# Three low parts and one block sum ahead of the first weight quad move from VectorE to GpSimd, and the order of the rest changes

## The reference, cut to what matters

```
def swiglu(h, wg, wu, wd):
    return (jax.nn.silu(h @ wg) * (h @ wu)) @ wd
...
xp = xp + swiglu(rmsnorm(xp, norm_ffn[l]), w_ff_gate[l], w_ff_up[l], w_ff_down[l])
```

## Time and profile before

| what | value |
|---|---|
| median of 3 runs | 2334.61 us |
| the profiled execution's span | 2334.1 us |
| its own time beside the span | no separate figure is given; the runs lie 0.8 us below to 1.3 us above the span |
| PE busy | 2267.3 us, 97% |
| DVE busy | 1309.4 us, 56% |
| POOL busy | 976.5 us, 42% |
| ACT busy | 862.2 us, 37% |

### The profile page before, as it was taken

One profiled execution on the slowest core, in us unless ns is written; L12 is line 12 of the kernel. 1 busy time (PEld: TensorE's weight loads), 2 busy tenths in 40 slices (PEclk: granted clock), 3 DMA queues, 4 the chain that ended last, 5 costly groups with the idle time before them and its releaser, 6 DMA issues.

```text
span 2334.1 us, 39824 instructions
## 1 busy us (share of the span) xinstructions
PE 2267.3 (97%) x15066; PEld 2183.7 (94%) x15066; DVE 1309.4 (56%) x2354; ACT 862.2 (37%) x1686; POOL 976.5 (42%) x988
## 2 busy tenths in 40 slices
PE   7999999999999899999999999999999989999997
PEld 7999998888999899999999999988889989999997
DVE  7996553334237835727589865433332387275374
ACT  4015233444213534625420152334441246255252
POOL 4544454232563342333455545533326623333231
PEclk9999999999999999999999999999999999999998
DMA  5251121111222222222234411211113312223121
GB/s 182 93 188 65 51 73 55 37 41 32 90 99 82 73 91 73 85 78 80 68 135 140 128 57 60 67 48 41 41 32 105 106 60 87 81 82 100 64 85 61
DMA packets 70564, 187.84 MB, mean 80 GB/s; under 512 B 19824, under 2 KB 22480, under 8 KB 69392
## 3 DMA queue, kind: packets, MB, share of 16 engines
q1 hardware_dynamic: 62608, 165.64, 21.9%
q10 hardware_dynamic: 7808, 20.16, 2.5%
HBM read 173.47 MB, written 14.14 MB: 80 GB/s over the span
## 4 chain that ended last, share of the span: by engine, by line
PE 91%; DVE 7%; ACT 1%; issue 1%; ACTq 0%; DMA 0%; SPq 0%; DVEq 0%
PE gemm L700 45%; PE gemm L1179 17%; PE gemm L1169 14%; PE side L1179 3%; PE side L1169 2%; PE side L1052 2%; PE side L1032 1%; PE side L815 1%; PE side L983 1%; PE side L1039 1%; DVE act_lo L2251 1%; PE side L903 1%; DVE prod L1996 1%; DVE prod L1833 1%; DVE x L1999 1%
## 5 line engine op out<-in xcount | busy, mean ns | idle before, releaser
L673 POOL TENSOR_TENSOR ring_lo<-w_raw,ring_hi 128x512 fp32r<-128x512 f32 x232 | 308.6, 1333 | 580.4 <-ACT ring_hi L1630 580.4
L654 POOL CAST w_hi<-w_raw 128x384 fp32r<-128x384 f32 x376 | 221.5, 589 | 717.9 <-PE gemm L700 681.9
L656 POOL TENSOR_TENSOR w_lo<-w_raw,w_hi 128x384 fp32r<-128x384 f32 x376 | 450.8, 1199 | 30.1
L700 PE MATMUL gemm<-h_hi,w_hi 128*128 128x320 f32 x1664 | 416.8, 332 | 6.3 <-DVE square L1825 4.2
L700 PE MATMUL gemm<-h_hi,w_lo 128*128 128x320 f32 x1664 | 379.8, 309 | 0.0
L700 PE MATMUL gemm<-h_lo,w_hi 128*128 128x320 f32 x1664 | 379.5, 309 | 0.0
L700 PEld LDWEIGHTS gemm<-h_hi,w_hi 128*128 128x128 f32 x1664 | 282.6, 189 | 36.9 <-issue 17.1
L1179 PE MATMUL gemm<-act_hi,ring_hi 128*128 128x320 f32 x960 | 300.1, 313 | 16.1 <-ACT gemm L1681 9.5
L1179 PE MATMUL gemm<-act_lo,ring_hi 128*128 128x320 f32 x960 | 299.4, 312 | 0.0
L1179 PE MATMUL gemm<-act_hi,ring_lo 128*128 128x320 f32 x960 | 299.4, 312 | 0.0
L700 PEld LDWEIGHTS gemm<-h_lo,w_hi 128*128 128x128 f32 x1664 | 278.7, 188 | 0.0
(11 more groups left out here) (318 smaller groups left out, 4321.9 us busy)
## 6 DMA issues: line engine op xcount, KB each, us to landing
w_raw<-in_ws_ff SPq DMA_DIRECT2D x120, 512.0 KB, 3.2
w_raw<-in_ws_gate SPq DMA_DIRECT2D x64, 512.0 KB, 3.3
w_raw<-in_ws_in SPq DMA_DIRECT2D x44, 512.0 KB, 3.3
w_raw<-in_ws_proj SPq DMA_DIRECT2D x64, 256.0 KB, 2.6
w_raw<-in_ws_out SPq DMA_DIRECT2D x16, 512.0 KB, 3.2
w_raw<-in_ws_fd SPq DMA_DIRECT2D x16, 384.0 KB, 3.0
x_park<-x ACTq DMA_DIRECT2D x2, 2560.0 KB, 12.4
x<-x_park ACTq DMA_DIRECT2D x4, 1280.0 KB, 6.2
```

The costliest lines, as they stand in the source:

```text
L654: eng.tensor_copy(w_hi[s][:, cols], w_raw[s][:, cols]).then_inc(w_high.sem, 1)
L656: eng.tensor_tensor(w_lo[s][:, cols], w_raw[s][:, cols], w_hi[s][:, cols].bitcast(F32), ALU.subtract).then_inc(w_split.sem, 1)
L673: eng.tensor_tensor(lo, src, hi.bitcast(F32), ALU.subtract).then_inc(lo_plain.sem, 1)
L700: mm = eng.matmul(dst[:, hf, 0:HALF], w, r[k][:, cols] if r in (xu_hi, xu_lo) else r[:, k, cols], start=first and k == 0 and part == 0, st ...
```

## The change

- A11 gets a buffer of its own (`a11_value`) on the place where the high part of S4 will lie, and S2 gets one (`s2_value`) on the place of `late`. So the low part of A11 and the sums that read A11 no longer exclude each other. S2 must now wait until S3 has read `late`, and the high part of S4 until the low part of A11 is made.
- POOL makes the low parts of A11, S3 and A22 and the sum S3: the low part of A11, the sum S3 and the low part of S3 ahead of operand 11's, and the low part of A22 ahead of operand 14's. Its low part of S3 waits for ACT's high part of S3.
- DVE makes block A22 right behind `late`, then S1, waits for S3 (`n_s3`), S2, block A12 and S4, and only then `up_out(1)`, the two `sum_low`, and the low parts of S2, A12, S1 and S4.
- ACT's order of high parts is A11, S3, A22, S2, S1, A12, S4; that of S3 stands behind cast 10 and the second silu (before: ahead of both).

```
+        act_value[A11], act_value[S2] = a11_value, s2_value
+        HIGH_ORDER = (A11, S3, A22, S2, S1, A12, S4)
+        POOL_LOW, DVE_LOW = (A11, S3, A22), (S2, A12, S1, S4)
...
                 for n, op in enumerate(FF_OPS):        (POOL)
+                    if n == 11:
+                        act_low(A11)
+                        eng.wait_ge(n_step.sem, n_step.at(l, 8))
+                        eng.tensor_tensor(af[S3][:, :, :], a11_value[:, :, :], late[:, :, :], ALU.subtract)\
+                           .then_inc(n_s3.sem, 1)
+                        act_low(S3)
+                    if n == 14:
+                        eng.wait_ge(n_step.sem, n_step.at(l, 13))
+                        act_low(A22)
...
                 cast(9)                                (ACT)
                 f_high(0, t2[1][:, :], 0)
-                act_high(S3, 9)
                 cast(10)
                 silu(1)
+                act_high(S3, 0)
                 cast(11)
-                act_high(S2, 15)
-                act_high(A12, 19)
-                act_high(S1, 14)
-                act_high(A22, 13)
-                act_high(S4, 20)
+                act_high(A22, 12)
+                act_high(S2, 14)
+                act_high(S1, 13)
+                act_high(A12, 18)
+                act_high(S4, 19)
...
                 gate_out(0)                            (DVE)
-                act_block(af[A11], 0, lo_half)
+                act_block(a11_value, 0, lo_half)
                 up_out(0)
                 act_block(late, 0, hi_half)
-                act_sum(af[S3][:, :, :], af[A11][:, :, :], late[:, :, :], ALU.subtract, 8)
+                act_block(af[A22], 4, hi_half)
                 f_low(0, t2[1][:, :], 0)
                 gate_out(1)
-                act_block(af[A22], 4, hi_half)
-                act_sum(af[S1][:, :, :], late[:, :, :], af[A22][:, :, :], ALU.add, 13)
-                act_sum(af[S2][:, :, :], af[S1][:, :, :], af[A11][:, :, :], ALU.subtract, 14)
+                act_sum(af[S1][:, :, :], late[:, :, :], af[A22][:, :, :], ALU.add, 12)
+
+                eng.wait_ge(n_s3.sem, n_s3.at(l, 1))
+                act_sum(s2_value[:, :, :], af[S1][:, :, :], a11_value[:, :, :], ALU.subtract, 13)
+                act_block(af[A12], 4, lo_half)
+                act_sum(af[S4][:, :, :], af[A12][:, :, :], s2_value[:, :, :], ALU.subtract, 18)
                 up_out(1)
-                act_low(A11)
-                act_low(S3)
                 sum_low(FF_QUADS[0] + 1)
-                act_block(af[A12], 4, lo_half)
                 sum_low(FF_QUADS[0] + 2)
-                act_sum(af[S4][:, :, :], af[A12][:, :, :], af[S2][:, :, :], ALU.subtract, 19)
-                for n in (S2, A12, S1, A22, S4):
+                for n in DVE_LOW:
                     act_low(n)
-                sum_low(FF_QUADS[0] + 4)
+                    if n == S1:
+                        sum_low(FF_QUADS[0] + 4)
```

More of the change, by code:

```diff
@@ L342, in encoder @@
         late, _ = sb("act_late", [P, 4, HALF], F32, sq_at)
+        s2_value, _ = sb("act_s2", [P, 4, HALF], F32, sq_at)
+        first_at = m_at + 2 * 2 * 4 * HALF * 4
+        a11_value, _ = sb("act_first", [P, 4, HALF], F32, first_at)
         A11, S3, S2, A12, S1, A22, S4 = range(7)
+        act_value = {n: af[n] for n in range(7)}
+        act_value[A11], act_value[S2] = a11_value, s2_value
+        HIGH_ORDER = (A11, S3, A22, S2, S1, A12, S4)
+        POOL_LOW, DVE_LOW = (A11, S3, A22), (S2, A12, S1, S4)
         u2, u4 = sq0[:, 0:HALF], sq0[:, HALF:T]
@@ L449, in encoder @@
         t_made = signal("weight_sums", 4 * N_QUADS)
-        n_step = signal("act_blocks", 20)
+        n_step = signal("act_blocks", 19)
+        n_s3 = signal("act_third_sum", 1)
         n_high = signal("act_high", 7)
-        n_split = signal("act_split", 7)
+        n_split = signal("act_split_dve", len(DVE_LOW))
+        n_split_pool = signal("act_split_pool", len(POOL_LOW))
         p_copy = signal("product_copied", 5 * N_QUADS)
@@ L668, in _, with act_low @@
                 pairs(A_UNITS // 2 + M_PAIRS, KT // 2, UW, UW)
+                def act_low(n):
+                    eng.wait_ge(n_high.sem, n_high.at(l, HIGH_ORDER.index(n) + 1))
+                    eng.tensor_tensor(al[n][:, :, :], act_value[n][:, :, :], ah[n][:, :, :].bitcast(F32), ALU.subtract)\
+                       .then_inc(n_split_pool.sem, 1)
                 for n, op in enumerate(FF_OPS):
+                    if n == 11:
[7 more added lines that the diff above has]
+                        act_low(A22)
                     if op.summed is None:
@@ L1187, in act @@
                     def act(i):
-                        if q == 0:
-                            eng.wait_ge(n_split.sem, n_split.at(l, i + 1))
+                        if q == 0 and i in POOL_LOW:
+                            eng.wait_ge(n_split_pool.sem, n_split_pool.at(l, POOL_LOW.index(i) + 1))
+                        elif q == 0:
+                            eng.wait_ge(n_split.sem, n_split.at(l, DVE_LOW.index(i) + 1))
                         return i
@@ L1658, in act_high @@
                 def act_high(n, made):
-                    eng.wait_ge(n_step.sem, n_step.at(l, made))
-                    eng.activation(ah[n][:, :, :], af[n][:, :, :], ACT.Copy).then_inc(n_high.sem, 1)
+                    if n == S3:
+                        eng.wait_ge(n_s3.sem, n_s3.at(l, 1))
+                    else:
+                        eng.wait_ge(n_step.sem, n_step.at(l, made))
+                    if n == S4:
+                        eng.wait_ge(n_split_pool.sem, n_split_pool.at(l, 1))
+                    eng.activation(ah[n][:, :, :], act_value[n][:, :, :], ACT.Copy).then_inc(n_high.sem, 1)
                 cast(6)
@@ L2249, in act_low @@
                 def act_low(n):
-                    eng.wait_ge(n_high.sem, n_high.at(l, n + 1))
-                    eng.tensor_tensor(al[n][:, :, :], af[n][:, :, :], ah[n][:, :, :].bitcast(F32), ALU.subtract)\
+                    eng.wait_ge(n_high.sem, n_high.at(l, HIGH_ORDER.index(n) + 1))
+                    eng.tensor_tensor(al[n][:, :, :], act_value[n][:, :, :], ah[n][:, :, :].bitcast(F32), ALU.subtract)\
                        .then_inc(n_split.sem, 1)
```

## The result

The changed kernel takes 2344.45 us, the median of 4 runs (2343.55 to 2345.24). The kernel before, beside it on the same chip, takes 2334.11 us. The ratio is 1.0046, with a 95% interval of 1.0034 to 1.0058: 10.3 us slower. The prediction had 2346.7 us, in a range of 2337 to 2351.

What follows compares the result with a forecast made beforehand. DVE's chain up to operand 13's low part was taken to bound PE's sixth product in each layer. 2 x 5.2 us plus 1.7 us for the clock gave +12.1 us on 2334.6: 2346.7 us, range 2337 to 2351.

Steps and rivals of the forecast that it cites:

- The bound: Each FFN's first quad: DVE's chain up to operand 13's low part sets PE's sixth block product; 25 us at stake.
- Step 1: DVE loses sum S3 (1.41 us) and three low parts (1.40 us each): 5.6 us less per layer.
- Step 2: Four 1280-column instructions added to POOL, 2.95 us each, cost DVE 2.8 us each: 11.2 us per layer.
- The 2.81 us: A 1280-column POOL instruction's length by the Trainium skill, in place of 2.95; it would give 2345.6 us.
- Step 3: DVE's idle 0.22 and 0.16 us go because `gate_out(1)` and `up_out(1)` come after their products: 0.4 us less per layer.
- The layout of the queues: Queues laid out from 743.6: operand 13's low part done at 781.1, 4.9 us behind 776.22.
- The sum of 5.2 us: Per layer, DVE's chain before the sixth product: +11.2 - 5.6 - 0.4 = +5.2 us.
- Step 5: A short PE idle before the sixth product lowers its clock in one of two layers: +1.7 us in all.
- Rival A: POOL's work lies in DVE's holes, so DVE's chain is 6.0 us shorter per layer: 2322.6 us; chance 0.12.
- Rival B: No change: each POOL instruction holds DVE about half its length, 1.5 us, 6.0 against 6.0 saved: 2334.6 us; chance 0.08.
- Rival C: Slower: wait before the sixth product lowers PE's clock in both layers, 6.8 instead of 1.7 us: 2351.8 us; chance 0.10.

Runs made afterwards that it cites:

- the reordered kernel: Kernel before, nothing moved to POOL; DVE makes operand 13's low part right behind A22's, ACT makes A12's and S4's high parts later: 2329.11 us, ratio 0.9983.
- the dose: Kernel before plus three unneeded 1280-column subtractions on POOL in front of operand 11's low part: 2348.55 us, ratio 1.0064.

## Why the prediction was right

- **The bound.** DVE's queue in front of the sixth product, twice: shown for the kernel before and the changed one. Taking 4.9 us of it away from the changed kernel and adding 7.4 to the kernel before moved the time by 8.0 and 14.5 us. Moving PE's idle time to another place moved the sixth product by 0.4 us, and the time by 2.6 to 3.6, of which the greater part is open. Once the queue was 5.4 us shorter, the bound was no longer there.
- **Step 1 (5.6 us off DVE)** stands: the instructions are gone, and back on DVE they advance its chain by 1.40 as before.
- **Step 2 (four times 2.8 us)** was a little high. The four cost DVE 2.71, 2.71, and with 1.0 for operand 11 taken from 6.27, two of 2.63: 10.7 in place of 11.2 us. The duration of 2.95, extrapolated from 384 and 512 columns, was too long itself: of the 3.21 us that S3 took on POOL from 748.68, 0.4 were waiting for DVE's first piece of A22, which leaves 2.8, and the three subtractions in a row follow each other by some 3.2 us with one piece of DVE of 0.46 between. The 2.81 us that the prediction worked out and set aside was the better value.
- **Step 3 (0.4 us of idle DVE)** stands for the two places: DVE has no idle time in front of either output now. In the window behind the plain units DVE idles 0.35 us all the same, where it was 0.24 before, so not all of the 0.4 was won.
- **The layout of the queues** had PE's second product near 769.7 and the sixth at 781.1 on the clock of the trace before; they came at 769.74 and 781.14, though the plain units ended 0.4 us later, so the interval was 0.4 to 0.5 us too long. The sum of 5.2 us, which I kept over the 4.9 of the layout, is 0.8 above the measured 4.4. The layout was the better of the two.
- **Step 5 (1.7 us for the clock)** was not paid at that place. Behind the sixth product of the changed kernel the clock was 1.00, in both layers of both its profiles; layer 0 of the first:

```profile
781.50:789.00 7.50, 7.50 (x54) 7.50 (x53) 5.68 (x11) 3.82 (x9) 1.30 (x1) 1.00 0.34 107
```

- **What the two windows don't explain.** 2 x 4.4 = 8.7 us, the profiled spans differ by 9.0 and the medians by 10.3. In the profiles the stretch ahead of the first FFN's wait is 0.4 us longer, the one between the waits 0.8 shorter and the one behind the second 0.7 longer. The time of a run is 1.8 us above its span wherever both are on record, so the profiled execution of the kernel before would be 1.8 us above its median and that of the changed kernel 0.5: that is the other 1.3. Runs of one kernel lie that far apart (2331.3 to 2337.6 for the kernel before in the second series). So the number came closer than its terms: 1.7 us for the clock that were not paid and 1.7 too much in the two sums stand against 1.6 us from outside the windows, which is luck.
- **Rival A** (POOL in DVE's holes) fell: each read on POOL cost 2.7 us. Its one row, the 3.61 us of operand 14 in the earlier trace rows, did show something real, that DVE can pass POOL by, but that delays POOL and does not make its work free. **Rival B** would have needed half that price. **Rival C** asked for the lower clock behind the sixth product in both layers. That happened in the kernel with the work back on DVE and not in the changed one.

## What to carry to other kernels

Before work is moved from VectorE to GpSimd, look in the timeline for VectorE instructions whose duration grows where GpSimd's lie over them. If both read two SBUF tiles, what is moved is paid at GpSimd's price, here 2.7 for 1.4 us, and the move only helps while VectorE idles, reads PSUM, or where GpSimd only writes. When a full queue sets the start of something, first take out of it what that start doesn't need: here this, with two of ACT's copies put off as well, gave 4 to 5 us, and nothing was moved to POOL. Then look again, because the bound has moved: 5.4 us came out of the queue in each layer, and 2.2 of them reached the next quad.

## What the runs showed that was not expected

- DVE can pass POOL by for long. In the reordered kernel operand 14's low part, 1.3 us of work, took 7.54 us while six instructions of DVE that began behind it went ahead, of 0.68 and 1.48 us, each ready when the one before ended; POOL got through at 770.9, where DVE seems to have waited for one of its own results. The same place took 7.66 and 7.72 us in the other windows. Elsewhere, as between the three subtractions of the dose, a waiting POOL came next after one instruction. What makes the difference is open.
- The length of a wait did not tell what the clock would do. In front of the sixth product, 2.34 us (the changed kernel) were followed by a clock of 1.00, and 3.19 us (work back on DVE) by 0.54; but the 1.83 us of the kernel with memsets, in layer 1, were followed by 0.60 (the third figure from the end):

```profile
1921.40:1925.10 3.70, 3.70 (x18) 3.70 (x17) 3.12 (x6) 0.99 (x2) 0.18 (x1) 0.60 0.42 142
```

  A change that moves a wait can so cost or win about 1.5 us in each stretch, 3 us in two layers, where the changes tested here are worth 4 to 15 us.
